# Prompt attention values in a hybrid decoder step: queries moved to the partitions of the value product

## The reference, cut to what matters

```python
s_s = jnp.einsum('bqgrd,bqgnkd->bqgrnk', qg, ks.astype(f32))
m_s = (pos <= tq[None, :, None, None, None]).reshape(B, Q, G, 1, -1)
p_s = masked_softmax(s_s.reshape(B, Q, G, R, -1), m_s).reshape(s_s.shape)
o_s = jnp.einsum('bqgrnk,bqgnkd->bqgrd', p_s, vs.astype(f32))
s_w = jnp.einsum('bqgrd,bwgd->bqgrw', qg, kw.astype(f32))
p_w = masked_softmax(s_w, m_w[None, :, None, None, :])
o_w = jnp.einsum('bqgrw,bwgd->bqgrd', p_w, vw.astype(f32))
g = gates.reshape(B, Q, G, R, 3)
o = g[..., 0:1] * o_c + g[..., 1:2] * o_s + g[..., 2:3] * o_w
```

## Time and profile before

| What | Value |
|---|---|
| Median of 3 runs | 1567.63 us (1562.02 to 1571.54) |
| The profiled execution's own time | 1563.48 us |
| Its span | 1561.7 us |
| TensorE busy | 1410.2 us, 90% |
| VectorE busy | 542.0 us, 35% |
| ScalarE busy | 422.5 us, 27% |
| Mean granted TensorE clock | 0.914 |
| The changed stage | 389.4 to 530.2 us of the span |

### The profile page before, as it was taken

One profiled execution on the slowest core, in us unless ns is written; L12 is line 12 of the kernel. 1 busy time (PEld: TensorE's weight loads), 2 busy tenths in 40 slices (PEclk: granted clock), 3 DMA queues, 4 the chain that ended last, 5 costly groups with the idle time before them and its releaser, 6 DMA issues.

```text
span 1561.7 us, 20717 instructions
## 1 busy us (share of the span) xinstructions
PE 1410.2 (90%) x7766; PEld 1109.8 (71%) x7766; DVE 542.0 (35%) x1425; ACT 422.5 (27%) x971; POOL 30.8 (2%) x77
## 2 busy tenths in 40 slices
PE   6899999597889898988898799969999999999995
PEld 4677777574556676766776677858888888878883
DVE  4200002628665664645465464251001001001114
ACT  3000004203443574555466453040000000000003
POOL 3000000000000000000000000000000000000000
PEclk9799999557786999999999999989999999999997
DMA  7433423100200315315523532132122122122201
GB/s 295 182 124 111 158 85 124 55 17 14 108 1 0 157 73 230 160 69 228 228 80 149 228 150 108 55 135 74 61 81 73 62 81 69 41 74 74 71 21 57
DMA packets 20823, 162.46 MB, mean 104 GB/s; under 512 B 2680, under 2 KB 6872, under 8 KB 10472
## 3 DMA queue, kind: packets, MB, share of 16 engines
q1 hardware_dynamic: 17896, 92.42, 16.3%
q0 software_dynamic: 2736, 69.36, 10.5%
q10 hardware_dynamic: 144, 0.04, 0.0%
HBM read 156.73 MB, written 9.24 MB: 106 GB/s over the span
## 4 chain that ended last, share of the span: by engine, by line
PE 76%; DMA 9%; DVE 8%; ACT 3%; issue 2%; POOL 0%; ACTq 0%; DVEq 0%
PE PS L272 69%; DMA ringreg<-in_cmp_dram,idx 4%; DMA creg<-in_cmp_dram,idx 4%; PE PS L921 2%; PE PS L747 2%; PE PS L792 1%; DVE ringreg L1551 1%; DMA trunk<-in_x_t_dram 1%; DVE smx L1764 1%; PE PS L840 1%; DVE zreg L1674 0%; DVE rstd L1311 0%; ACT sreg L1065 0%; DVE creg L1493 0%; POOL sreg L469 0%
## 5 line engine op out<-in xcount | busy, mean ns | idle before, releaser
L272 PE MATMUL PS<-creg,ringreg 128*128 128x272 f32 (+2 forms) x2160 | 514.2, 401 | 11.7 <-DVE creg L1377 5.4
L272 PEld LDWEIGHTS PS<-creg,ringreg 128*128 128x128 f32 (+2 forms) x2160 | 410.2, 191 | 108.4 <-issue 10.9
L272 PE MATMUL PS<-zreg,ringreg 128*128 128x272 f32 (+5 forms) x864 | 223.7, 419 | 11.6 <-ACT ringreg L1140 6.4
L272 PEld LDWEIGHTS PS<-zreg,ringreg 128*128 128x128 f32 (+1 forms) x864 | 165.2, 202 | 57.3 <-issue 14.9
L272 PE MATMUL PS<-zreg,w 128*128 128x256 f32 (+2 forms) x544 | 141.1, 390 | 11.7 <-DVE zreg L1676 5.7
L272 PEld LDWEIGHTS PS<-zreg,w 128*128 128x128 f32 (+1 forms) x544 | 90.4, 187 | 31.7 <-DVE zreg L1676 11.0
L1183 ACT ACTIVATE zreg<-PS 128x512 f32<-128x512 f32 x128 | 75.8, 592 | 69.8 <-PE PS L747 69.6
L921 PE MATMUL PS<-ident,sreg 128*128 128x128 f32 x288 | 49.0, 337 | 36.9 <-ACT hxs L1195 36.9
L1032 ACT ACTIVATE sreg<-mixreg 128x544 f32<-128x544 f32 x24 | 15.2, 657 | 247.7 <-DVE mixreg L1305 235.6
L272 PE MATMUL PS<-zreg 128*128 128x256 f32 x256 | 77.4, 384 | 1.6 <-ACT hxs L1195 1.6
L921 PEld LDWEIGHTS PS<-ident,sreg 128*128 128x128 f32 x288 | 43.3, 176 | 47.8 <-ACT hxs L1195 39.3
(11 more groups left out here) (303 smaller groups left out, 1438.4 us busy)
## 6 DMA issues: line engine op xcount, KB each, us to landing
ringreg<-in_w_ada_dram SPq DMA_DIRECT2D x24, 1024.0 KB, 6.2
ringreg<-in_w_f_dram SPq DMA_DIRECT2D x22, 1024.0 KB, 4.8
ringreg<-in_w_in_dram SPq DMA_DIRECT2D x11, 1024.0 KB, 4.8
ringreg<-in_w_f_dram SPq DMA_DIRECT2D x16, 704.0 KB, 4.0
sreg<-in_win_dram SPq DMA_DIRECT2D x8, 512.0 KB
ringreg<-in_w_o_dram SPq DMA_DIRECT2D x4, 1024.0 KB, 9.3
out_dram<-in_win_dram SPq DMA_DIRECT2D x1, 4064.0 KB
trunk<-in_x_t_dram SPq DMA_DIRECT2D x1, 2176.0 KB, 9.1
```

The source lines that it names most:

```text
L272: return nc.tensor.matmul(o, lhsT, rhs, start=start, stop=stop, **kw)
```

## The change

The value product is turned round. The transposed exponentials, 128 keys by 128 queries, are now the stationary operand and the 64 value columns stream through, so that the result has its queries on the partitions. There the factor gate / sum is one number for each partition. The exponentials are no longer scaled in place; the transposes wait for the exponentials alone. The two branches no longer add up in PSUM: each of the four results of a pair (two groups, two branches) has 64 columns of its own in one bank, and VectorE's new `rows` scales and adds them into a 128 x 128 tile `orow`. A new TensorE step, `back`, transposes that tile once for both groups, and `output` adds 128 x 128 to MIXT, once for a pair. The sums and factors of a pair are kept together in `pst`, which is double-buffered by pair; `scale` treats both groups at once.

```diff
             def turned(i, t):
...
-                    pe.wait_ge(sem("nsa_p"), i * 32 + 2 * t + q + 1)
+                    pe.wait_ge(sem("nsa_exp"), i * 32 + 2 * t + q + 1)
...
             def values(i, t):
...
-                if t >= 2:
-                    pe.wait_ge(sem("nsa_out"), i * 16 + t)
-                o = PS[g * HD:(g + 1) * HD, 4 + g, 0:P]
+                if g == 0 and n >= 2:
+                    pe.wait_ge(sem("nsa_out"), i * 8 + n)
                 for q, c in ((0, 768 + P), (1, 1024 + P)):
+                    o = PS[:, 4 + n % 2, g * P + q * HD:g * P + (q + 1) * HD]
                     for k in range(j + 1):
-                        last = matmul(o, VT[:, k, c + g * HD:c + (g + 1) * HD], pt[:, (4 * q + k) * P:(4 * q + k + 1) * P],
-                                      q == 0 and k == 0, q == 1 and k == j)
+                        last = matmul(o, pt[:, (4 * q + k) * P:(4 * q + k + 1) * P], VT[:, k, c + g * HD:c + (g + 1) * HD], k == 0, k == j)
                 last.then_inc(sem("nsa_pv"), 1)
+
+            def back(i, n):
+
+                pe.wait_ge(sem("nsa_o"), i * 8 + n + 1)
+                nc.tensor.transpose(PS[:, 4 + n % 2, 2 * P:3 * P], orow[n % 2], ident[:, :]).then_inc(sem("nsa_ot"), 1)
...
                     turned(i, t)
+                    if t >= 3 and t % 2 == 1:
+                        back(i, t // 2 - 1)
                 values(i, 15)
+                back(i, 7)
...
-                def finish(t):
...
-                    for q in range(2):
-                        v = PB[t % 3][:, q * LP:q * LP + w]
-                        nc.vector.tensor_scalar(v, v, st[:, 3, q:q + 1], None, ALU.mult).then_inc(sem("nsa_p"), 1)
...
+                def rows(n):
+
+                    st = pst[:, n % 2]
+                    dve.wait_ge(sem("nsa_pv"), i * 16 + 2 * (n + 1))
+                    o, v = orow[n % 2], PS[:, 4 + n % 2, :]
+                    for g in range(G):
+                        lk(nc.vector.tensor_scalar(o[:, g * HD:(g + 1) * HD], v[:, g * P:g * P + HD], st[:, 3, g, 0:1], None, ALU.mult))
+                    for g in range(G):
+                        last = nc.vector.scalar_tensor_tensor(out=o[:, g * HD:(g + 1) * HD], in0=v[:, g * P + HD:(g + 1) * P],
+                                                              scalar=st[:, 3, g, 1:2], in1=o[:, g * HD:(g + 1) * HD], op0=ALU.mult, op1=ALU.add)
+                        if g == 0:
+                            lk(last)
+                    last.then_inc(sem("nsa_o"), 1)
...
+                for n in range(8):
+                    if n < 7:
+                        prepare(2 * n + 2)
+                    scale(n)
+                    if n < 7:
+                        prepare(2 * n + 3)
+                    if n >= 1:
+                        rows(n - 1)
+                        output(n - 1)
+                rows(7)
+                output(7)
```

More of the change, by code:

```diff
@@ L222, in build @@
         qcur = RR[:, 5120:5120 + 2 * LP].rearrange("p (r t) -> p r t", r=2)
-        pst = RR[:, 6144:6144 + 2 * 8].rearrange("p (b k j) -> p b k j", b=2, k=4)
-        gpc = RR[:, 6160:6160 + 2 * TT * 6].rearrange("p (r t c) -> p r t c", r=2, t=TT)
+        pst = RR[:, 6144:6144 + 2 * 16].rearrange("p (b k g j) -> p b k g j", b=2, k=4, g=G)
+        gpc = RR[:, 6176:6176 + 2 * TT * 6].rearrange("p (r t c) -> p r t c", r=2, t=TT)
+        orow = [RR[:, 6400 + b * P:6400 + (b + 1) * P] for b in range(2)]
         PCW = R * TT * NCP
@@ L815, in _ @@
             with pe.Fori(0, R // 2) as i:
-                pe.wait_ge(sem("nsa_out"), i * 16 + 1)
+                pe.wait_ge(sem("nsa_out"), i * 8 + 1)
                 pe.wait_ge(sem("nsa_q"), i * 2 + 2)
@@ L1134, in exponentials @@
                     nc.scalar.activation(PB[t % 3][:, q * LP:q * LP + w], PS[:, 2 * g + q, 0:w], ACT.Exp, scale=HD ** -0.5,
-                                         bias=pst[:, g, 1, q:q + 1], accum_out=pst[:, g, 2, q:q + 1]).then_inc(sem("nsa_exp"), 1)
+                                         bias=pst[:, t // 2 % 2, 1, g, q:q + 1], accum_out=pst[:, t // 2 % 2, 2, g, q:q + 1]
+                                         ).then_inc(sem("nsa_exp"), 1)
             with act.Fori(0, R // 2) as i:
-                act.wait_ge(sem("nsa_out"), i * 16 + 1)
+                act.wait_ge(sem("nsa_out"), i * 8 + 1)
                 for h in range(2):
@@ L1562, in _ @@
             base = step[0]
-            PER = 2 + 16 * 5
+            PER = 2 + 16 * 2 + 8 * 6
             with dve.Fori(0, R // 2) as i:
@@ L1577, in prepare @@
                     w = (j + 1) * P
-                    st = pst[:, g]
+                    st = pst[:, t // 2 % 2, :, g]
                     dve.wait_ge(sem("nsa_sc"), i * 16 + t + 1)
@@ L1598, in output @@
[L1598 to L1602, removed]
-                prepare(0)
[L1605 to L1610, removed]
@@ L1611, in _, with scale @@
-                output(14)
-                output(15)
+                def scale(n):
+                    st = pst[:, n % 2]
+                    dve.wait_ge(sem("nsa_exp"), i * 32 + 4 * (n + 1))
+                    lk(nc.vector.tensor_scalar(st[:, 2], st[:, 2], 1e-30, None, ALU.max))
+                    lk(nc.vector.reciprocal(st[:, 2], st[:, 2]))
+                    lk(nc.vector.tensor_tensor(st[:, 3], st[:, 2], gpc[:, n // 4, n % TT, :].rearrange("p (g c) -> p g c", g=G)[:, :, 1:3], ALU.mult))
@@ new lines, in output @@
+                def output(n):
+                    dve.wait_ge(sem("nsa_ot"), i * 8 + n + 1)
+                    o = MIXT[:, bass.ds(i * 2 + 4 + n // 4, 1), n % TT * P:(n % TT + 1) * P].rearrange("p o t -> p (o t)")
+                    nc.vector.tensor_tensor(o, o, PS[:, 4 + n % 2, 2 * P:3 * P], ALU.add).then_inc(sem("nsa_out"), 1)
+                prepare(0)
+                prepare(1)
+                for n in range(8):
[7 more added lines that the diff above has]
+                        output(n - 1)
@@ L1613, in _ @@
+                rows(7)
+                output(7)
                 assert count[0] == PER, count[0]
             step[0] += PER * (R // 2)
-            dve.wait_ge(sem("nsa_out"), 8 * R + 1)
+            dve.wait_ge(sem("nsa_out"), 4 * R + 1)
             for r in range(R):
```

2 lines of the change are left out of this document (1 added, 1 removed).

## The result

| | before | after |
|---|---|---|
| median | 1569.59 us (1562.02 to 1572.97, 4 runs) | 1628.58 us (1624.42 to 1632.89, 4 runs) |
| ratio | 1 | 1.0383 [1.0335, 1.0431] |
| profiled span, mean granted clock | 1561.7 us, 0.914 | 1626.8 us, 0.872 |

The account below looks back on a forecast made before the run. TensorE, and the level of its clock, was taken as the bound. 67 - 3 + 10 - 8 = +66 us on the profiled 1563.5 us gave 1629.5, named as 1630 us, with a range of 1573 to 1648.

Parts of the forecast that it names:

- The scaling removed, 0 to -2 us: VectorE's 64 in-place scalings, 21.8 us of work, go; TensorE was not found waiting for them, so 0 to -2 us.
- The price of a value record, unchanged: 320 value records on TensorE stream half the columns but keep their spacing; 0 to -6 us, taken as 0.
- The clock, +67 - 3 - 8: Stage mostly at 1.2 GHz: 67 us more TensorE work, -3 for waits partly covered, -8 for short rises.
- factor of 0.90: Extra time for TensorE's 74.7 busy us in the 2.4 GHz stretches if run at 1.2 GHz: 67 us more.
- Structure at 1.2 GHz, +10: Added work and waits at the low clock: 6 us back transposes, 1 us waits for rows, 3 us pass ends.
- Structure alone, 12 us: Cost with the clock where it is today: 4 + 9 x 0.7 + 3 - 1 = 12 us.
- rival 1: The clock rises where it rises today, so structure alone decides: about 1576 us, range 1568 to 1584; chance 0.16.
- 9 x 0.7: TensorE's mid-pass waits for VectorE's rows: 9 us for both passes at 2.4 GHz, reduced because part runs at 1.2 GHz.
- The likeliest case: Clock low for most of the stage: 1630 us, own range 1610 to 1648; chance 0.62.
- rival 2: The clock rises in one pass or late in both, so half of the 67 us is paid: about 1607 us; chance 0.12.
- Rival 3: Narrow value records are really half as long, saving 16 us: about 1559 us; chance 0.10 together with Rival 4.
- Rival 4: The new code removes a wait the profile charges to others: about 1566 us; chance 0.10 together with Rival 3.

Follow-up runs that it names:

- e3_noscale: The kernel before, without VectorE's 64 in-place scalings of the exponentials; 1562.33 us, ratio 0.9986.
- e1_wide: The changed kernel with each value product streaming 128 value columns instead of 64, transpose back in the same step; 1587.87 us, ratio 1.0132.
- e2_mid: The changed kernel with each value product streaming 96 value columns instead of 64; 1600.21 us, ratio 1.0211.
- e9_half: The kernel before, with value products streaming only 64 of the 128 queries behind a load of 64 columns; 1556.04 us, ratio 0.9924.
- e10_narrow_late: The changed kernel, still 64 streamed columns, with the transpose back one step later in TensorE's order; 1624.82 us, ratio 1.0374.
- e4_late: e1_wide with the transpose back one step later in TensorE's order; 1564.74 us, ratio 0.9981 to the kernel before.

## Why the prediction was right

**What bounds the kernel.** Right: TensorE, and through it the clock's level. TensorE is busy 59.0 us more and idle 4.7 us more, which makes the 63.7 us.

**The scaling removed, 0 to -2 us.** Right within what e3_noscale can tell: 0.9986 [0.9959, 1.0013].

**The price of a value record, unchanged.** Right: 1.97 us for eight at the low clock in both shapes; 0.11 us each at the high one.

**The clock, +67 - 3 - 8.** Right in its main cause and near in size. It was low for all but 10.3 us of the stage, where two rises of 7 us were foreseen. By the prediction's own factor of 0.90 these two would have given back 12.6 us and not 8; the 10.3 us that came give 9.3. e1_wide and e2_mid show by the dose that the streamed columns are a cause, and that with fewer of them the clock rises later. The argument had been that half as many columns are streamed in the same time. e9_half narrows it: the 64 columns do not keep the clock down where the load is as narrow, so it is 64 columns behind a load twice as wide that matter. The prediction did not see the second part, that the wait for VectorE's rows ends a high stretch: the first one ends at 446.8, in the wait of 1.79 us, and without such a wait one execution of e10_narrow_late took 1604.96 us.

**Structure at 1.2 GHz, +10.** The transposes were put at 6 us, and 16 of them take 7.0 (modelled ends). The waits were put at 1 + 3 us, and four waits come to 5.6: one of 1.79 in the first pass's last short step, one of 1.12 in the second's, and 1.34 at each pass's end. That is 12.6 against 10. The four linked operations take 1.2 us, not 1.0.

**Structure alone, 12 us: too small.** This was rival 1's sum, 1576 us, and e1_wide, which has that structure with wide records, takes 1588. Its terms hold one by one, the 16 transposes at 5.5 us (with modelled ends) instead of 4. For the mid-pass waits the sum had 9 x 0.7 = 6.3 us; in the trace of e1_wide they are two of 1.74 and three of 0.94, 6.3 us. Pass ends wait 1.34 and 1.33. The step that failed is "with the clock where it is today": a wait of 1.7 us behind short steps was priced at its own length, and it also took the clock down for the 10.3 us after it in the first pass and for 23.9 us in the second. The likeliest case did not rest on this; the changed kernel had little high clock left to lose.

**The number.** That 1630 is within 2 us of 1628.58 is partly luck. With the terms as they were measured, 12.6 for 10 and 9.3 for 8, the sum is 67.3 us, against 63.7 in the trace, so that the first two terms (67 and -3) are together some 4 us too large. And the sum stood on one execution of 1563.48 us, while the median of before is 1569.59: by the medians the change costs 59 us, not 66.

**The rivals.** Rival 1 (clock as today) and rival 2 (half of it) are out by the stretches: 0.53. Rival 3, records half as long, is out by the timeline, though e9_half shows that records 0.06 us apart do exist, where the load is narrow as well. Rival 4, a hidden wait removed, is out by e3_noscale. What would show it came as written (TensorE busy for 90% of the stage, clock 0.53), but for the wait of L812 at the low clock, foreseen as near none and found at 1.12 us in one short step.

What stays open is the amount of streaming that the clock wants. The runs order the mixtures and give no bound.

## What to carry to other kernels

When a product is turned, ask of each record not only how long it takes but how much of that time the array streams: here 64 moving columns behind a load of 128 took the time of 128 moving columns, and the clock rose late or not at all. Let the wider side stream, put work of at least two steps between a producer on another engine and the transpose that waits for it, and price a wait like the 1.4 to 1.8 us here, between short steps of a dense loop, as a possible fall of the clock and not only at its own length. Where a loop enters at the low clock, a few wide products that nobody reads, put where TensorE waits anyway, can be worth more than the edit in question: here 1.5%.

## What the runs showed that was not expected

- The best kernels measured are before with filler products, 1545.85 us (1543.54 to 1548.70), and the turned form with wide records, late transposes and filler products, 1547.51 us. The first does 6 wide products a pass more than before, and is 1.5% faster.
- Rise and fall went with different things here: the fewer columns were streamed, the later the clock rose; a wait of 1.38 to 1.79 us between short steps stands at each of the seven falls in mid-pass.
- TensorE was busy without a gap and stayed at 1.2 GHz: 10.30 of 10.30 us in e1_wide from 436.8, in which long scores of 64 rows, value records and transposes alternate. In e4_late the same kinds of work go on for 44.4 us at the high level once it has risen.
- Records of 64 moving columns start 0.06 us apart behind a load of 64 columns and 0.11 us apart behind a load of 128.
- The executions of e10_narrow_late scatter over 25 us, and its mean granted clocks go with them. That a pass more or less catches the rise is the likely reason, but only one of them was traced. In e4_late the ten executions lie within 12 us, and the four of the changed kernel, where almost nothing of the stage is at the high clock, within 9.
